# A hybrid decoder layer on one core: the preparation stage is carried into the first four steps of the mixers

## The reference, cut to what matters

```
u  = RMSNorm_pre(x)                                  # x: 2048 x 1024, f32
p  = u @ W_in                                        # columns: rg_x, rg_gate, q, k, v, o (512 each), i, f (4 each)
y_rg = RMSNorm(RG-LRU(conv4(rg_x)) * gelu(rg_gate))
y_ml = headRMSNorm(sigmoid(o) * mLSTM(silu(conv4(q)), silu(conv4(k)), v, log_i, log_f))   # 4 heads
x  = x + RMSNorm_post(concat(y_rg, y_ml) @ W_out)
x  = x + RMSNorm_post(relu(RMSNorm_pre(x) @ W_up)^2 @ W_down)
```

## Time and profile before

| | |
|---|---|
| median of the runs | 2466.69 us |
| the profiled execution | 2467.44 us |
| its span | 2465.6 us |
| share of the span busy: PE, DVE, ACT, POOL | 95%, 52%, 26%, 34% |
| granted clock of TensorE, mean | 0.972 |
| HBM read, written | 201.67 MB, 50.40 MB |

### The profile page before, as it was taken

The page is one execution under the profiler, slowest core; times in us unless marked ns, Lnnn a source line. Parts: engine busy times, 40 slices in busy tenths (PEclk is TensorE's granted clock), DMA queues, the critical chain, the costliest instruction groups (busy, mean ns, idle before and its releaser), DMA issues.

```text
span 2465.6 us, 29981 instructions
## 1 busy us (share of the span) xinstructions
PE 2335.1 (95%) x10696; PEld 1943.9 (79%) x10696; DVE 1278.3 (52%) x1584; ACT 642.5 (26%) x1159; POOL 834.4 (34%) x486
## 2 busy tenths in 40 slices
PE   5779999999999599999999999979899999999998
PEld 5758888888887487888888888868688888888886
DVE  5345665656656256445435444517755434534535
ACT  3315554545545232001101101114201101100112
POOL 8400000000000108536435534610746534633630
PEclk9689999999999799999999999989899999999999
DMA  4634453635542552112111101327412111101203
GB/s 171 245 119 153 149 190 121 218 122 174 165 165 71 170 163 94 43 52 68 34 43 60 51 34 51 102 98 244 144 51 69 43 42 51 60 27 50 68 17 145
DMA packets 125177, 254.85 MB, mean 103 GB/s; under 512 B 8105, under 2 KB 43137, under 8 KB 125121
## 3 DMA queue, kind: packets, MB, share of 16 engines
q1 hardware_dynamic: 97008, 157.37, 19.0%
q0 software_dynamic: 24320, 88.35, 11.4%
q10 hardware_dynamic: 3792, 8.47, 0.9%
HBM read 201.67 MB, written 50.40 MB: 102 GB/s over the span
## 4 chain that ended last, share of the span: by engine, by line
PE 60%; DVE 3%; issue 1%; ACT 1%; DMA 1%; POOL 0%; ACTq 0%; DVEq 0%; SPq 0%; PEldq 0%; POOLq 0%
PE o_ps L1350 20%; PE o_ps L1352 20%; PE o_ps L1351 20%; DVE o_relu L1626 1%; DVE o_ff_lo L1630 1%; ACT o_ps L1451 1%; PE o_ps L1374 0%; DMA o_v_lo<-ylo_d 0%; DVE o_acc L1570 0%; DVE o_v_lo L1619 0%; DMA o_w_raw<-in_w_out 0%; DVE o_h_t L1586 0%; ACT o_ff_hi L1508 0%; DVE o_h_t L1599 0%; DVE o_v_t L1607 0%
## 5 line engine op out<-in xcount | busy, mean ns | idle before, releaser
L1319 POOL TENSOR_TENSOR w_hi<-o_w_raw,one 128x1024 fp32r<-128x1024 f32 x100 | 191.7, 1917 | 685.2 <-PE o_ps L1352 594.7
L1350 PE MATMUL o_ps<-o_v_hi,w_hi 128*128 128x512 f32 x1024 | 400.1, 391 | 4.8 <-DVE o_v_lo L1619 4.8
L1351 PE MATMUL o_ps<-o_v_lo,w_hi 128*128 128x512 f32 x1024 | 399.6, 390 | 0.0
L1352 PE MATMUL o_ps<-o_v_hi,w_lo 128*128 128x512 f32 x1024 | 399.6, 390 | 0.0
L1640 DVE TENSOR_TENSOR o_acc<-o_ps,o_acc 128x512 f32<-128x512 f32 x224 | 154.2, 690 | 377.5 <-PE o_ps L1352 377.2
L658 PE MATMUL m_unit_ps<-u_hi,w_hi 128*128 128x512 f32 x768 | 309.4, 403 | 6.3 <-issue 6.3
L1626 DVE TENSOR_TENSOR o_relu<-o_relu 128x512 f32<-128x512 f32 x128 | 218.8, 1710 | 182.7 <-ACT o_relu L1505 181.7
L1505 ACT ACTIVATE o_relu<-o_ps 128x512 f32<-128x512 f32 x128 | 76.5, 597 | 874.9 <-PE o_ps L1352 843.3
L658 PE MATMUL m_unit_ps<-u_hi,w_lo 128*128 128x512 f32 x768 | 301.5, 393 | 0.0
L658 PE MATMUL m_unit_ps<-u_lo,w_hi 128*128 128x512 f32 x768 | 299.9, 390 | 0.0
L1630 DVE TENSOR_TENSOR o_ff_lo<-o_relu,o_ff_hi 128x512 fp32r<-128x512 f32 x128 | 243.1, 1899 | 90.8 <-ACT o_ff_hi L1508 90.8
(11 more groups left out here) (255 smaller groups left out, 3639.5 us busy)
## 6 DMA issues: line engine op xcount, KB each, us to landing
o_w_raw<-in_mlp_w_up POOLq DMA_DIRECT2D x64, 512.0 KB, 4.7
o_w_raw<-in_mlp_w_down POOLq DMA_DIRECT2D x64, 512.0 KB, 3.6
u_hi<-uhi_d SPq DMA_DIRECT2D x14, 2048.0 KB, 10.6
u_lo<-ulo_d SPq DMA_DIRECT2D x14, 2048.0 KB, 15.0
w_raw<-in_w_in POOLq DMA_DIRECT2D x24, 512.0 KB, 4.8
p_xu<-in_x SPq DMA_DIRECT2D x16, 512.0 KB, 7.9
uhi_d<-u_hi SPq DMA_DIRECT2D x4, 2048.0 KB, 7.5
ulo_d<-u_lo SPq DMA_DIRECT2D x4, 2048.0 KB, 13.1
```

What stands on the lines that cost most here:

```text
L1319: pool.tensor_tensor(w_hi[i], w_raw[i % 2][:], one_bc, ALU.mult).then_inc(w_split[i], 1)
L1350: nc.tensor.matmul(dst, sh, mh, start=(i == 0), stop=False)
L1351: nc.tensor.matmul(dst, sh, ml, start=False, stop=False)
L1352: last = nc.tensor.matmul(dst, sl, mh, start=False, stop=(i == n - 1))
```

## The change

build_prepare and the barrier behind it are gone. What it did is done in build_mixers:

- The first four tiles of x are loaded by SP into SBUF (x_first), squared and then scaled by rstd on ScalarE (root_x: a copy with a scale per partition), transposed by TensorE (transpose_x, four tiles of one block of 128 channels into one bank), and the two parts of u are taken from the bank with the gain as a scale per partition: high by ScalarE, low by DVE (high_of_x, low_of_x).
- The x tiles of t = 1, 2, 3 are prepared in periods t - 1. GpSimd's queue loads them, into the three w_raw buffers and x_extra; for t = 1 after the splits of the first six weights. Their 32 transposes follow units x, o and g, in groups of 3, 3 and 2 blocks (gap_tiles). SP stores the parts of each tile (store_u).
- Periods 0 to 3 begin with gate_unit: the gate columns of W_in, in two parts, are the stationary operand, and u the moving one, 24 products with 8 output partitions and 512 columns. ScalarE copies the result, GpSimd brings it through DRAM into 16 rows (gate_rows), and the chain over 4 chunks per head goes in four pieces of DVE work: gate_absolute, chunk_locals, chunk_maxima (with the running maxima handed on in m_carry), chunk_rows. TensorE's small transposes for it stand after units k, o and g (chain). load_rows stores e1 and e2 for periods 0 to 3, waits for that and loads gate_w in four transfers from the inputs.
- DVE's decay_arguments moves behind the convolution of q, weigh_queries ahead of weigh_scores. The mask is one block, read four times over; `ones` is one column.
- TensorE's loop starts at period 6, ScalarE's at 8, SP's at 4; the periods before are written out.

The diff, cut to its core, in the order SP, GpSimd, TensorE, ScalarE's period, DVE's period:

```diff
             def load_u(p, b):
                 sp.wait_ge(s["mm_g"], s.ready(p - 2))
+                if isinstance(p, int):
+                    sp.wait_ge(u_out[b], 64)
...
+            def store_u(t):
+                sp.wait_ge(ulo_made, KT * (t + 1))
+                for dst, src in ((k["uhi_d"], u_hi), (k["ulo_d"], u_lo)):
+                    sp.dma_start(dst[:, :, t * TILE:(t + 1) * TILE], src[:, t % 2].bitcast(F32)).then_inc(u_out[t % 2], 16)
             def load_rows(p):
...
+                if isinstance(p, int) and p < NT:
+                    sp.wait_ge(const_made, 8)
+                    sp.wait_ge(rows_made, p + 1)
...
+                    sp.wait_ge(rows_out, 32 * (p + 1))
...
+            store_u(0)
             load_rows(0)
+            store_u(1)
+            load_rows(1)
+            store_u(2)
+            store(0)
+            load_rows(2)
+            store_u(3)
+            load_u(4, 0)
+            store(1)
+            load_rows(3)
+            load_u(5, 1)
+            store(2)
+            load_rows(4)
+            store(3)
+            with sp.Fori(2, STEPS // 2 - 1) as j:
...
+            def load_x(t):
+                pool.wait_ge(squared, CPT * t)
+                if t == 1:
+                    for u in "xog":
+                        pool.wait_ge(w_split[u], 2)
+                else:
+                    pool.wait_ge(x_tr, KT * t)
+                for i in range(CPT):
+                    pool.dma_start(x_tile(t, i), a["x"][0, (t * CPT + i) * P:(t * CPT + i + 1) * P, :]).then_inc(x_in[i], 16)
...
+            for t in range(NT - 1):
+                load_x(t + 1)
+                gate_rows(t)
+            pool.wait_ge(x_tr, KT * NT)
             for c in range(3):
                 load_raw(c, 1)
+            gate_rows(NT - 1)
...
             def gates_and_transposes(m):
...
+                if isinstance(m, int) and m < NT - 1:
+                    pe.wait_ge(if_copied, m + 2)
...
+            def transpose_x(t, c):
+                pe.wait_ge(scaled, CPT * (t + 1))
+                if t and c % 3 == 0:
+                    pe.wait_ge(s[("xv", "xx", "xo")[c // 3]], s.ready(t - 1))
+                if t and c in (4, 5, 7):
+                    pe.wait_ge(ulo_made, KT * t + {4: 2, 5: 3, 7: 6}[c])
...
+            for p in range(NT):
+                gate_unit(p)
+                for n, u in enumerate(UNITS):
+                    unit(u, p, p % 2)
+                    if p:
+                        slots[n](p - 1)
+                    chain(p, n)
+                    if p < NT - 1:
+                        for c in gap_tiles.get(n, ()):
+                            transpose_x(p + 1, c)
...
                 if mix:
                     sigmoids_1(m)
+                if gates:
+                    copy_gates(p)
+                if prepare:
+                    squares(p + 1)
                 if project:
                     take("q")
...
                 if mix:
                     exponentials(m, g_m)
+                if gates:
+                    gate_exponential(p)
+                if isinstance(p, int) and 0 < p <= NT:
+                    floor_columns(p - 1)
+                if prepare:
+                    root_x(p + 1)
...
                     weigh_values(m)
+                    weigh_queries(m)
+                if gates:
+                    gate_absolute(p)
+                if prepare:
+                    inverse_rms(p + 1)
+                if mix:
                     weigh_scores(m)
-                    weigh_queries(m)
...
                     states(m)
+                if gates:
+                    chunk_locals(p)
+                if mix:
                     recurrence(m)
...
                 if mix:
                     head_numerator(m)
                 low_of("v")
+                low_parts_x(3)
                 if project:
                     convolve("x", p, g_p)
                     keep_history(p)
+                if gates:
+                    chunk_maxima(p)
                 if mix:
                     rg_output(m, g_m)
                     head_total(m)
                     head_output(m)
+                low_parts_x(4)
                 low_of("x")
                 if mix:
                     rg_square_sums(m)
                     rg_low(m)
+                if gates:
+                    chunk_rows(p)
+                low_parts_x(5)
```

More of the change, by code:

```diff
@@ new lines, in _ @@
+            pool.wait_ge(ident_made, 1)
+            pool.affine_select(out=k["ident"][:], in_=k["ident"][:], compare_op=ALU.not_equal, fill=1.0,
+                               base=0, pattern=[[-1, P]], channel_multiplier=1).then_inc(ident_made, 1)
+            for c in range(3):
+                load_first(c)
+            pool.memset(k["one"][:], 1.0).then_inc(const_made, 1)
+            pool.memset(k["mask"][:], BIG).then_inc(const_made, 1)
+            pool.memset(k["ones"][:], 1.0).then_inc(const_made, 1)
@@ new lines, in gate_unit @@
+            def gate_unit(p):
+                pe.wait_ge(ulo_made, KT * (p + 1))
+                if p:
+                    pe.wait_ge(prev_made, p)
+                for c in range(KT):
+                    for z, (w, x) in enumerate(((wif_hi, u_hi), (wif_hi, u_lo), (wif_lo, u_hi))):
+                        last = nc.tensor.matmul(n_ps[0:2 * NG, :], w[:, c, :], x[:, p % 2, c, :],
+                                                start=(c == 0 and z == 0), stop=(c == KT - 1 and z == 2))
+                last.then_inc(if_mm, 1)
@@ L737, in _ @@
+            for p in (NT, NT + 1):
+                for n, u in enumerate(UNITS):
+                    unit(u, p, p % 2, 32)
+                    slots[n](p - 1)
+                    if p == NT:
+                        chain(p, n)
+            with pe.Fori(0, (STEPS - NT) // 2 - 1) as j:
+                for b in range(2):
+                    p = j * 2 + (NT + 2 + b)
                     for n, u in enumerate(UNITS):
-                        unit(u, p, b)
+                        unit(u, p, b, j * 32 + 64)
@@ L1083, in low_of, with low_parts_x @@
                         split_low(u, g_p)
+                gates = isinstance(p, int) and p < NT
+                prepare = isinstance(p, int) and p < NT - 1
+                def low_parts_x(n):
+                    if prepare:
+                        for c in gap_tiles[n]:
+                            low_of_x(p + 1, c)
                 if mix:
-                    decay_arguments(m)
                     if before is not None:
@@ L1094, in period @@
                 if mix:
+                    decay_arguments(m)
                     gate_input(m)
```

671 lines of the change are left out of this document (288 added, 383 removed), and 9 rows, old and new, of the table base.

## The result

The kernel with the change takes 2486.93 us (median of four runs, 2485.16 to 2489.17) where the kernel before, on the same chip, takes 2467.0. The ratio is 1.0079, 95% interval 1.0067 to 1.0092: slower by 0.8%. The forecast was 2480.8 us and slower. The profiled execution took 2486.36 us, its span is 2484.7.

What follows compares the result with a forecast made beforehand. TensorE, with work for 95% of the span, was taken as the bound. Terms 80.5+61.3+70+74.4+57+11.6 = 354.8 put step 5 14.1 us later than 340.7, giving 2480.8 us; range 2438 to 2502.

Steps and rivals of the forecast that it cites:

- The start, 28: First gate product on TensorE, after x's first tiles are prepared: starts at 28 us, bounds 25 and 33.
- Step 0: First mixer step: TensorE stands 4.3 us before x's transposes and again at the end; step 1 starts at 80.5.
- The ends of steps 1 and 2: Last low parts of x finish after TensorE's work, at 61.3 against 51.2; TensorE stands 5.4 us at each end.
- chunk_locals: VectorE work of 6.4 us ahead of recurrence and head_numerator: slot 4 starts at 45.8, TensorE stalls 3.7 us.
- The stall of 1.1 for the numerators: Steps 1 and 2: VectorE finishes the states at 33.5 us into the step, so TensorE stalls 1.1 us.
- The queue of SP: y's stores behind u's 4 MB transfers delay ScalarE's g2 to 18.5, 31 and 26.5 us into steps 2, 3 and 4.
- rows stored, waited for, four gate_w loads, rows: 4.1: SP's work at the start of step 2 before its bulk store of u: 4.1 us.
- Cold starts: Slow TensorE clock after standing, 1.8 to 2.8 us each: 11.6 us together in steps 0 to 4, bounds 3 and 18.
- After step 5: 0: Four gate_w loads replace one per step and SP's queue has room: 0 us, bounds 0 and 3.
- (a): Rival: y's stores come in time and g2 never waits; step 5 starts at 314, 2440 us; chance 0.21.
- (b): Rival: waits as told but each shorter, since copies overlap, 15 to 20 us less; about 2463 us; chance 0.17.
- (c): Stalls feed on each other, five slow-clock units: 2505 us; sign: over 20 us at clock 0.5, 80 to 350; chance 0.12.

Runs made afterwards that it cites:

- Experiment 6: On experiment 1 plus edit 4: VectorE takes x's last low parts ahead of rg_square_sums, rg_low and chunk_rows; 2430.65 us, ratio 0.9853.
- experiment 8: On top of Experiment 6: chunk_locals moved behind head_numerator and the first low parts of u; 2430.23 us, ratio 0.9846.
- experiment 1: Kernel with the change, but each store of y on SP moved ahead of u's next store and loads; 2439.58 us, ratio 0.9884.
- experiment 3: Kernel with the change, but y_rg's stores for steps 2 to 4 issued on ScalarE's queue at SP's turn; 2464.62 us, one execution.
- Edits 2: Kernel with the change, but y's stores moved ahead of the loads of u only, still behind u's stores; 2465.88 us, one execution.
- edit 4: Kernel with the change, but gate_w's four loads moved ahead of SP's wait for rows_made in steps 0 to 3; 2478.26 us, ratio 1.0045.
- experiments 6 and 7: The second of these: kernel with the change, only the last two low parts of u ahead of rg_low and chunk_rows; 2484.49 us, ratio 1.0064.
- kernel 9: On top of Experiment 6: y_rg's pair of stores issued ahead of the rows and the wait for rows_made; 2412.03 us, ratio 0.9772.

## Why the prediction was right, and where it was off

- **The start, 28.** Measured 29.15, within 25 to 33. The scalings end at 19.4 (17.8 forecast), the last transposes at 25.3 (25). What the gate product then waits for isn't the last part of x but the low part of W_in's gate columns: the subtraction of 128 by 64 elements at L1132 takes 1.72 us, from 27.34. It ends at 29.06, 0.1 us behind a split of weights on GpSimd (27.06 to 28.96). Three passes of 128 by 4 behind it on VectorE took 1.98, 1.59 and 2.25 us, and each of them too ended within 0.1 us of a split's end; two others among them took 0.18 and 0.16, and so did those after GpSimd's last split (40.07). So it looks as if VectorE waited for GpSimd here; no experiment isolates it.
- **Step 0.** 53.5 forecast, 50.8 measured. The wait at its end was put at 2.7 and is 2.24. That ahead of x's transposes was 4.3 and is 2.63 (at 60.85 us, ended by ScalarE's copy of v).
- **The ends of steps 1 and 2,** 5.4 each: 5.24 each. Experiment 6 shows that moving the low parts takes 7.3 us of these waits away.
- **chunk_locals,** a stall of 3.7 in slot 4: 2.37 in step 1, 2.38 in step 2 and 4.2 in step 3. The cause was right, since experiment 8 turns the wait into one for chunk_locals' own result. The stall of 1.1 for the numerators is not in the list of waits.
- **The queue of SP.** The largest term, right in kind and too small in size: 45.7 us of TensorE's waits by the sum, 51.5 measured. Slot 0's waits were 8.9 and 21.4 (19.8 less 10.9, 32.3 less 10.9) and are 11.9 and 23.4; the scores' wait was 8.8 and is 9.0; gate_w's 6.6 and is 7.2. g2 itself was put 18.5, 31 and 26.5 us into its step and came at 23.0, 34.6 and 29.6. The step that failed is "rows stored, waited for, four gate_w loads, rows: 4.1": up to the store of u these took 6.4 us. The rows' stores needed 3.1 us to land (140.69 to 143.84), and the five issues behind them 3.1. This is 2.3 of the 4.5 us by which g2 was late in step 2; the rest is the transfers, put at 14.4 (1.3, 10.3, 1.3 and 1.5) and 16.5 long from the issue of the store of u (146.97) to g2 (163.50). Slot 0 waited less than g2 was late, since TensorE, with its cold first unit, came to slot 0 at 12.4 us and not at 10.9.
- **Cold starts,** 11.6 with bounds of 3 and 18: the term that was missed most, about 21. Rows of the steps 1 to 4 and of one window within step 2, kernel after (columns as in rows 4):

```profile
79.95:140.53 60.58, 52.93 (x265) 41.07 (x266) 37.30 (x88) 35.03 (x65) 4.10 (x8) 0.97 0.37 134
140.53:218.83 78.30, 58.74 (x265) 44.36 (x266) 37.89 (x89) 33.89 (x63) 4.21 (x6) 0.85 0.27 100
218.83:300.64 81.81, 54.16 (x234) 40.09 (x234) 34.80 (x74) 21.71 (x43) 5.16 (x7) 0.79 0.45 152
300.64:362.45 61.81, 45.65 (x206) 36.33 (x206) 27.66 (x54) 20.12 (x42) 1.77 (x2) 0.86 0.38 127
...
200.00:205.00 5.00, 4.30 (x23) 4.26 (x24) 4.59 (x13) 2.41 (x8) 0.00 (x0) 0.62 0.00 0
```

Two estimates agree on it. What is left of each step's length after the prediction's own work (45.5, 51.2, 51.2, 47.2, 41.2) and the measured waits is 21.2 us. TensorE's busy time in windows of 1 us, times what their clock lacks to 1.00, comes to 23.8 in these five steps, of which the sum held 2.8 within its 45.5.

| step | waits: forecast | measured | cold starts: forecast | left over |
|---|---|---|---|---|
| 0 | 7.0 | 4.9 | 1.0 | 0.4 |
| 1 | 10.1 | 7.6 | 2.3 | 1.8 |
| 2 | 18.8 | 19.5 | 2.3 | 7.6 |
| 3 | 27.2 | 27.7 | 3.5 | 7.0 |
| 4 | 15.8 | 16.2 | 2.5 | 4.5 |

So steps 2, 3 and 4 came out 6.0, 3.9 and 2.3 us longer than forecast almost wholly by the clock: their waits were told to within 0.7 us each, though the parts were not (slot 0's were longer, those told for the numerators and slot 4, 4.8 together, shorter). In step 2 the clock was low behind the stall of slot 0, as forecast, and again at 200 us behind a wait of only 2.38 us for den2, which the sum held for nothing but its length. The waits told for step 3 add up to 73.4 with its work, and not to the 74.4 of the sum.
- **After step 5: 0.** Measured -2.7, outside the bounds of 0 and 3 on the good side, but no more than single runs of one kernel differ by.
- **The rivals.** (a), y's stores in time, was priced at 2440; the order that makes it true gave 2439.6 (experiment 1); to agree within 1 us is luck, since the cold starts of that kernel are as mis-sized as here (about 20 us by the same estimate, where the rival holds 7.6). It decided at the point named, the landing of y behind 4 and 8 MB. The reason to give it 0.21 only was the order in the code, and experiment 3 bears this out: on its own queue the pair was there 6.8 us sooner, still late. (b) took part with 3 us of waits fewer than told. (c) took part with the clock, some 10 us more than the sum held, of the 24 that its 2505 asks for. Its sign was met: from 80 to 350 us the mean granted clock is 0.85, which makes some 80 us at 0.5 (an estimate, twice 0.15 of 270), with TensorE busy in about half of them, where more than 20 was to show (c). But the sign doesn't tell the rivals apart, since it counts standing time too and is met in experiment 1 as well (some 44 us).

Total: 354.8 forecast for step 5, 362.45 measured, 7.7 too low: 1.2 at the start and 9.6 of clock, less 3.1 of waits. The late gain of 2.7 hides a part, and the forecast's time was 6.1 us low, 0.25%. The mechanism, y's stores behind the bulk of u on SP's queue, is shown by experiments 1 to 3. That the number came so close is in part luck, since a term that was almost 10 us off was met by others off the other way.

What stays open: why the steps behind step 5 come out slightly shorter, beyond the 1.3 us of the mixers. Edits 2 and 3 were run once, so their times are good to a few us only; the waits in their traces carry the argument. Why the clock falls behind a short wait in one run and not in another is open too, and so is what edit 4 is worth on top of edit 1 (some 3 to 6 us).

## What to carry to other kernels

When work is moved from ahead of a loop into its first rounds, write down for each queue that it passes what now stands behind what. A small store whose buffer is wanted again soon was best issued ahead of every bulk transfer, and ahead of a wait for a slow producer, on its queue: the order of a few lines was worth 46 us here, and putting the store ahead of the rows another 19, where TensorE's busy time fell by 17. And a stall removed ahead of such a wait is given back at the wait (experiments 6 and 7): look first for what the next wait is pinned to.

## What the runs showed of the hardware

- An issue can itself take long. Behind the 4 MB of a store of u, SP's issue of a 256 KB store took 5.50 us in step 2, and the loads of u issued behind it in step 3 5.17 and 5.01 (225.99 and 231.21), where an issue on an empty queue takes 0.38. All that SP had to do next, waits for other semaphores too, stood behind it.
- A second queue helps a small transfer only in part: from the first issue to g2, half a megabyte on ScalarE's queue beside 4 MB on SP's took 8.3 us (8.9 in step 3), against 15.2 behind them on one queue and 2.8 in the earlier trace rows.
- A short wait can cost more in clock than in length, and not the same each time. Behind den2's wait of 2.36 to 2.38 us the granted clock fell to 0.66 from 125 to 130 us in the kernel after, to 0.57 and 0.75 in two such windows in kernel 1, to 0.62 from 200 to 205 us in the kernel after, and not at all in step 2 of kernel 9. The same step 1 took 60.5 or 63.7 us by it.
- From kernel 6 to 9, 21.2 us were won in three steps with 11.8 us of waits gone. From the kernel after to experiment 1, TensorE's waits from 0 to 400 us fell by 43.7 us (98.8 to 55.1) and the span by 45.9.
- Three passes of 128 by 4 on VectorE (at 29.47, 31.70 and 33.52 us, kernel after) took 1.98, 1.59 and 2.25 us and ended within 0.1 us of a weight split on GpSimd; behind the last split such passes took 0.16 to 0.17.
